# Convolution blocks of a streaming encoder trunk in halves: their matmul form, their order, their banks, and the decay differences on GpSimd

## The chip, the cores and the metric

One core of one Trainium2 chip, one launch. The metric is the device time of the launch in microseconds (us). The kernel is written against the engines directly: every engine has its own instruction stream, and semaphores order them. TensorE is PE in the profile, VectorE DVE, ScalarE ACT, GpSimd POOL, SyncE SP.

## What is computed

A trunk of four layers on 256 tokens of width 1024, all float32, with a memory of 256 tokens. Layers 0 and 3 have a state-space mixer, layer 1 differential attention, layer 2 spatial gating; each has cross attention to the memory beside its mixer, and a feed-forward part behind it:

```python
for i in range(DEPTH):
    h = rmsnorm(x, norm_mix[i])
    proj = h @ w_in                       # mixer input and the cross queries
    mix_out = mixer(proj)                 # by the kind of layer
    cross = memory_cross_attention(xq, mem_n, w_mem_kv[i], ...)
    x = x + jnp.concatenate([mix_out, cross], axis=-1) @ w_out
    x = x + squared_relu_mlp(rmsnorm(x, norm_ffn[i]), w_ff1[i], w_ff2[i])

def mamba2_mixer(proj, ...):
    z, xbc, dt = jnp.split(proj, ...)     # 2048, 4096, 32 columns
    xbc = jax.nn.silu(causal_depthwise_conv(xbc, conv_w, conv_b))   # 4 taps
    xs, bm, cm = jnp.split(xbc, ...)      # 2048, 1024, 1024
    dt = jax.nn.softplus(dt + dt_bias)
    y = ssd_chunked(xs, dt, a, bm, cm) + d_skip * xs
    return grouped_rmsnorm(y * silu(z))

def segsum_exp(a):                        # inside ssd_chunked
    cs = jnp.cumsum(a, axis=-1)
    return jnp.exp(jnp.where(mask, cs[..., :, None] - cs[..., None, :], -jnp.inf))
```

The convolution runs along the tokens, over 4096 channels: 32 tiles of 128 channels. The differences of `cs` under the exponential are what "decay differences" means below.

## The kernel before, in words

**Weights as a stream.** All weights come in 569 units of 512 KB (128 partitions x 1024 numbers) and one small dt unit. For each unit SP issues a DMA into the ring `raw` (6 slots), ACT casts it into `w_hi_t` (ring of 4, L1434), DVE subtracts to make the low part `w_lo_t` (L1678), and PE multiplies. Each float32 product is a sum of three matmuls: high by high, high weight by low activation, low weight by high activation. All partial sums stand in PSUM, 8 banks of 128 x 512 numbers: stream blocks take the pairs (0, 1) and (2, 3) in turn, small work takes one of the banks 4 to 7.

**Three forms of a unit.** *nat* (L1229 to L1240) gives tokens on partitions: 2 K tiles x 2 token tiles x 3 products = 12 matmuls of 128x512 a unit. *feat* (L1241 to L1249), used for the convolution blocks alone, gives channels on partitions: 2 K tiles x 4 channel tiles x 3 products = 24 matmuls of 128x256 a unit. *wide* (L1250 to L1266), used by the first feed-forward product, has the high and the low activations side by side in `hT2`, so that one 128x512 matmul gives high by high in the left half of a bank and high by low in the right half, and a 128x256 one adds low by high: 8 + 8 matmuls a unit. Every form moves 6144 columns a unit.

**The order of the work.** The class `Plan` writes one list of steps before the kernel is built; each engine's stream is that list, cut to its own part. `unit` (L224) adds a weight unit, and threads (Python generators) place small steps between units: `yield n` waits n units, `yield n, "kind"` waits on while that kind's engine is estimated to be late (`is_late`, by the table `COST`: ACT, DVE and PE time of each step). `stream_job` takes the next bank pair and forces steps to be placed until its former contents have been read.

**A convolution block** (`conv_block` in `ssm`, 8 a layer, 4 units each, 512 channels) fills one bank pair. Step "conv", once for each half of the block: ACT writes tap 0 with the bias from PSUM into `xsT` or `bcT` (two Identity operations 128x256, L1537), and DVE adds the other three taps from PSUM (six SCALAR_TENSOR_TENSOR, L1761). The pair is free when DVE is through with the second half. Then "silu" on ACT, and for the xs blocks "xs_turn", transposes on PE.

**The decay differences** ("ssd_gap", 8 groups a layer) are 8 TENSOR_SCALAR of 128x128 a group on DVE (L1791) on data that a DMA brings. POOL makes dt ("dt_soft", L1132 to L1148), `xdt` and `xs` weights ("ssd_xd", L1149 to L1162) and the reciprocal roots of the norms.

**Around it.** The blocks of a state-space layer have a fixed order (the tuple in `ssm`: bc16, bc24, xs0, z0, xs1, ...). `key(0, 0)`, the first key block of the memory, takes the pair (0, 1), which value block 0 has to leave first. `head` does a cross attention head: x_score, x_exp, x_norm, x_turn, x_out. `out_projection` goes over its tiles and, for each, over the two column halves `a` and `b`.

Of the kernel before, what the change touches and what calls it, by code (L numbers as in the profile page):

```python
# [53 lines left out]
for _name, _w in (("norm_mix", DEPTH * 8), ("norm_ffn", DEPTH * 8), ("mem_norm", 8), ("xq", DEPTH * 2), ("xk", DEPTH * 2),  # L54
# [14 lines left out]
    "evac": (1.2, 0, 0), "conv": (1.0, 2.7, 0), "silu": (1.1, 0, 0), "xs_turn": (1.2, 0, 0.9), "dt": (0, 0.4, 0), "dt_turn": (0.3, 0.7, 0.2),  # L69
    "dt_soft": (0, 0.8, 0), "decay": (0.3, 0, 0.4), "ssd_gap": (0, 1.7, 0), "ssd_xd": (0, 0, 0), "ssd_a": (1.5, 0.6, 0.65), "ssd_m": (0, 1.8, 0), "ssd_b": (0, 0.85, 2.2),  # L70
# [41 lines left out]
class Plan:  # L112
# [3 lines left out]
    def __init__(self):  # L116
# [6 lines left out]
        self.low_later = self.ticks = 0  # L123
        self.norm_ahead = False
# [97 lines left out]
    def unit(self, form, src, weight, job, first, last, part, at=None, nf=0, then=None):  # L222
# [12 lines left out]
        self.work(1.06, 1.23 * on, {"feat": 2.88, "wide": 2.78}.get(form, 2.72))  # L235
# [77 lines left out]
    def key(self, i, n):  # L313
        self.normed("mem", ("w_mem_kv", i), n * COLS, 2, ("m", self.r_m), "kT", n, ("xk", i))
# [18 lines left out]
    def head(self, i, h):  # L333
# [150 lines left out]
    def out_projection(self, i, l, kind, order):  # L484
# [68 lines left out]
    def ssm(self, i, l):  # L553
# [32 lines left out]

        def conv_block(ft):
            job = self.stream_job(True, True)

            def taps():  # L590
                if 0 < ft < 16:
                    self.until(lambda: ft // 4 - 1 in xs_act)
                self.step("conv", l=l, ft=ft, half=0, job=job, n=self.count("conv"))
                self.spawn(silu(job, ft))
            self.block("feat", "hT", w, DIN + ft * P, job, taps)
# [72 lines left out]
        for what, k in (("bc", 16), ("bc", 24), ("xs", 0), ("z", 0), ("xs", 1), ("bc", 20), ("z", 1), ("bc", 28), ("q", 0), ("xs", 2), ("z", 2),  # L668
# [166 lines left out]
def bass_trunk(nc, A, out):  # L835
    plan = Plan()
    steps, NU = plan.steps, len(plan.units)
    ctx = ExitStack()
    with ctx:
# [59 lines left out]
        xsT = sb("xsT", [P, 4, SEQ], F32, o_s1)  # L899
# [1120 lines left out]
```

## Time and profile before

| what | us |
| --- | --- |
| median of 3 runs (1770.59 to 1770.93) | 1770.88 |
| the profiled execution | 1770.17 |
| its span | 1768.40 |
| PE busy | 1760.0 |
| DVE busy | 1182.3 |
| ACT busy | 1005.3 |
| POOL busy | 220.0 |

The profiled execution is 0.71 us under the median, and 1.77 us of its time lie outside the span. There are 26013 instructions. "Busy" is the union of an engine's instructions; a matmul's own length in the timeline (0.28 us for 128x256) overlaps its neighbours', so the pace of PE is read from the distance of starts, and a row marked "xN" holds N instructions from its start on. A number in square brackets at the end of a timeline row is the idle time before the instruction, and what ended it.

### The profile page before, as it was taken

What the parts mean: (1) busy time and instruction counts of PE and PEld (TensorE: products, weight loads), DVE (VectorE), ACT (ScalarE), POOL (GpSimd) and SP (SyncE); (2) the same over time, 40 slices, a digit from 0 to 9 for tenths busy, and PEclk for the clock granted to TensorE, in tenths of its full rate; (3) what the DMA queues carried; (4) which work ended last, traced back from release to release, by engine and by line L of the source; (5) the groups of instructions that cost most, each with busy time, mean ns of one, the idle gap of its engine ahead of it and who ended that gap; (6) DMA issues with size and microseconds to landing.
All of it is one profiled execution on the core that took longest, in us unless ns stands there. A gap on an engine that the chain in (4) does not pass through costs nothing.

```text
span 1768.4 us, 26013 instructions
## 1 busy us (share of the span) xinstructions
PE 1760.0 (100%) x9556; PEld 1518.9 (86%) x9556; DVE 1182.3 (67%) x1628; ACT 1005.3 (57%) x1598; POOL 220.0 (12%) x548
## 2 busy tenths in 40 slices
PE   9999999999999999999999999999999999999999
PEld 8998988888888888888888888888899998888887
DVE  5788876666665666656566566655678887656665
ACT  6667775544455675544465545444566777545443
POOL 2412231000012220000012300000131223100000
PEclk9999999999999999999999999999999999999999
DMA  7555543555555443555565445555557554355554
GB/s 271 171 204 186 179 143 122 181 190 191 191 186 180 156 141 121 177 191 191 191 213 180 160 136 182 191 191 191 190 168 215 177 173 150 122 190 189 191 191 143
DMA packets 90041, 314.03 MB, mean 178 GB/s; under 512 B 10176, under 2 KB 11584, under 8 KB 89920
## 3 DMA queue, kind: packets, MB, share of 16 engines
q1 hardware_dynamic: 89328, 311.27, 53.0%
q8 instruction: 80, 1.31, 0.3%
q10 hardware_dynamic: 592, 1.12, 0.2%
q14 instruction: 41, 0.34, 0.1%
HBM read 311.23 MB, written 1.11 MB: 177 GB/s over the span
## 4 chain that ended last, share of the span: by engine, by line
PE 96%; DVE 3%; ACT 1%; issue 1%; ACTq 0%; DVEq 0%
PE ps L1236 19%; PE ps L1238 19%; PE ps L1237 19%; PE ps L1258 13%; PE ps L1265 7%; PE ps L1247 3%; PE ps L1248 3%; PE ps L1249 3%; PE ps L1283 1%; PE ps L1383 1%; PE ps L1334 1%; PE ps L1293 1%; DVE w_lo_t L1678 1%; DVE xsT L1761 1%; DVE bcT L1761 1%
## 5 line engine op out<-in xcount | busy, mean ns | idle before, releaser
L1678 DVE TENSOR_TENSOR w_lo_t<-raw,w_hi_t 128x1024 fp32r<-128x1024 f32 x569 | 691.7, 1225 | 367.6 <-ACT w_hi_t L1434 367.0
L1434 ACT ACTIVATE w_hi_t<-raw 128x1024 fp32r<-128x1024 f32 x569 | 596.9, 1059 | 393.5 <-PE ps L1238 148.5
L1236 PE MATMUL ps<-w_hi_t,act_hi 128*128 128x512 f32 x832 | 327.7, 394 | 0.6 <-issue 0.6
L1237 PE MATMUL ps<-w_lo_t,act_hi 128*128 128x512 f32 x832 | 324.3, 390 | 0.0
L1238 PE MATMUL ps<-w_hi_t,act_lo 128*128 128x512 f32 x832 | 324.1, 390 | 0.0
L1258 PE MATMUL ps<-hT,w_hi_t 128*128 128x512 f32 x1024 | 256.0, 392 | 0.0
L1258 PEld LDWEIGHTS ps<-hT,w_hi_t 128*128 128x128 f32 x1024 | 185.9, 189 | 34.4
L1238 PEld LDWEIGHTS ps<-w_hi_t,act_lo 128*128 128x128 f32 x832 | 156.2, 188 | 33.1
L1236 PEld LDWEIGHTS ps<-w_hi_t,act_hi 128*128 128x128 f32 x832 | 156.4, 188 | 31.6 <-issue 1.0
L1237 PEld LDWEIGHTS ps<-w_lo_t,act_hi 128*128 128x128 f32 x832 | 156.5, 188 | 30.2
L1236 PE MATMUL ps<-w_hi_t,hT 128*128 128x512 f32 x416 | 165.7, 398 | 0.0
L1238 PE MATMUL ps<-w_hi_t,hT 128*128 128x512 f32 x416 | 162.4, 390 | 0.0
L1237 PE MATMUL ps<-w_lo_t,hT 128*128 128x512 f32 x416 | 162.1, 390 | 0.0
L1247 PE MATMUL ps<-hT,w_hi_t 128*128 128x256 f32 x512 | 149.1, 291 | 0.5 <-DVE w_lo_t L1678 0.5
L1265 PEld LDWEIGHTS ps<-hT,w_lo_t 128*128 128x128 f32 x1024 | 139.7, 190 | 10.0
L1249 PE MATMUL ps<-hT,w_lo_t 128*128 128x256 f32 x512 | 144.9, 283 | 0.0
L1248 PE MATMUL ps<-hT,w_hi_t 128*128 128x256 f32 x512 | 144.8, 283 | 0.0
L1265 PE MATMUL ps<-hT,w_lo_t 128*128 128x256 f32 x1024 | 142.8, 282 | 0.0
L1236 PE MATMUL ps<-w_hi_t,memT_hi 128*128 128x512 f32 x252 | 101.5, 403 | 0.9 <-issue 0.8
L1247 PEld LDWEIGHTS ps<-hT,w_hi_t 128*128 128x128 f32 x512 | 98.1, 192 | 2.1 <-issue 1.6
L1248 PEld LDWEIGHTS ps<-hT,w_hi_t 128*128 128x128 f32 x512 | 98.2, 192 | 0.4
L1238 PE MATMUL ps<-w_hi_t,memT_lo 128*128 128x512 f32 x252 | 98.5, 391 | 0.0
(225 smaller groups left out, 2279.2 us busy)
## 6 DMA issues: line engine op xcount, KB each, us to landing
raw<-in_wstream SPq DMA_DIRECT2D x569, 512.0 KB, 3.3
gap<-cs_rows SPq DMA_DIRECT2D x32, 256.0 KB, 4.8
mix<-in_mem SPq DMA_DIRECT2D x4, 256.0 KB, 5.2
x<-in_x SPq DMA_DIRECT2D x1, 1024.0 KB, 9.1
raw<-in_wstream SPq DMA_DIRECT2D x2, 256.0 KB, 4.1
wsT<-in_sgu_wT ACTq DMA_DIRECT2D x1, 512.0 KB, 3.6
sgain<-in_sgu_gain ACTq DMA_DIRECT2D x1, 512.0 KB, 5.9
out<-x SPq DMA_DIRECT2D x1, 512.0 KB, 2.8
```

The costliest lines, as they stand in the source:

```text
L1236: pe.matmul(o, ah, wh[:, n], start=first and c == 0, stop=False)
L1237: pe.matmul(o, ah, wl[:, n], start=False, stop=False)
L1238: mm = pe.matmul(o, al, wh[:, n], start=False, stop=last and c == UK - 1)
L1247: pe.matmul(o, wh[:, n], ah, start=first and c == 0 and f % 2 == 0, stop=False, skip_group_check=True)
L1248: pe.matmul(o, wh[:, n], al, start=False, stop=False, skip_group_check=True)
L1249: mm = pe.matmul(o, wl[:, n], ah, start=False, stop=last and c == UK - 1, skip_group_check=True)
L1258: pe.matmul(o.rearrange("p (a b) -> p a b", a=2), wh[:, n], hT2[:, :, kt, :], start=first and c == 0, stop=False, skip_group_check=True)
L1265: mm = pe.matmul(o[:, 0:SEQ], wl[:, n], hT2[:, 0, kt, :], start=False, stop=last and c == UK - 1, skip_group_check=True)
L1283: mm = pe.transpose(ps[:, bf, f * SEQ + t * P:f * SEQ + (t + 1) * P], src[:, t, (2 * m + f) * P:(2 * m + f + 1) * P], ident)
L1434: act.activation(w_hi_t[:, u % RING, :], raw[:, u % SLOTS, :], ACT.Copy).then_inc(w_hi, 1)
L1678: dve.tensor_tensor(w_lo_t[:, u % SLOTS, :], raw[:, u % SLOTS, :], w_hi_t[:, u % RING, :].bitcast(F32), ALU.subtract)\
L1761: ins = dve.scalar_tensor_tensor(out=dst[:, f, d:SEQ], in0=ps[:, job.banks[h], (f % 2) * SEQ:(f % 2 + 1) * SEQ - d], scalar=col("conv_w", ...
```

## The change

1. The form "feat" goes; a form "half" takes its place. A convolution block is now two halves of 256 channels, each of two units and with a bank pair of its own. A unit is 4 K tiles x 256 channels instead of 2 K tiles x 512, brought by two DMAs of 256 KB from two of the old units, in rows of 1 KB. PE does 8 matmuls of 128x512 (high weight by high and low activations side by side) and 8 of 128x256. There are 512 matmuls fewer in the program.
2. The step "conv" is cut in two. "conv_sum": ACT copies the two right halves (high by low) of the pair into a buffer `cv` (128x512), DVE adds the left halves to it, and the banks are free; then POOL writes tap 0 with the bias from `cv` into `xsT` or `bcT` (two TENSOR_SCALAR 128x256). "conv": DVE's six operations read `cv`, not PSUM. conv_sum is placed with the work of one unit earlier (`w=len(self.units) - 1`).
3. "ssd_gap" runs on POOL, and its cost in the table is 0.
4. The order of the blocks starts with z0; x_out comes two units after x_turn; key(0, 0) uses the banks (6, 7); the out projection begins with both first tiles for `a`, then for `b`.

```diff
-    "evac": (1.2, 0, 0), "conv": (1.0, 2.7, 0), "silu": (1.1, 0, 0), ...
-    "dt_soft": (0, 0.8, 0), "decay": (0.3, 0, 0.4), "ssd_gap": (0, 1.7, 0), ...
+    "evac": (1.2, 0, 0), "conv_sum": (0.65, 0.7, 0), "conv": (0, 2.7, 0), "silu": (1.1, 0, 0), ...
+    "dt_soft": (0, 0.8, 0), "decay": (0.3, 0, 0.4), "ssd_gap": (0, 0, 0), ...
...
     def key(self, i, n):
-        self.normed("mem", ("w_mem_kv", i), n * COLS, 2, ("m", self.r_m), "kT", n, ("xk", i))
+        self.normed("mem", ("w_mem_kv", i), n * COLS, 2, ("m", self.r_m), "kT", n, ("xk", i), (6, 7) if i == n == 0 else None)
...
         self.step("x_turn", n=n, job=pT)
-        yield 1, "x_out"
+        yield 2, "x_out"
...
-        for n in range(last):
+        for n, nb in ((0, 0), (1, 0), (0, 1), (1, 1)):
+            unit(n, (a, b)[nb], nb, False, None)
+        for n in range(2, last):
...
+        def half_summed(ft, half, job):
+            if 0 < ft < 16 and half == 0:
+                self.until(lambda: ft // 4 - 1 in xs_act)
+            n = self.count("conv")
+            self.until(lambda: n < 3 or self.n.get("taps", 0) >= n - 2)
+            job.read_act(self)
+            job.read_dve(self)
+            self.step("conv_sum", w=len(self.units) - 1, l=l, ft=ft, half=half, job=job, n=n, xs_free=...)
+            self.spawn(taps(ft, half, n))
...
-        for what, k in (("bc", 16), ("bc", 24), ("xs", 0), ("z", 0), ("xs", 1), ("bc", 20), ("z", 1), ("bc", 28), ("q", 0), ("xs", 2), ("z", 2),
+        for what, k in (("z", 0), ("bc", 16), ("bc", 24), ("xs", 0), ("z", 1), ("xs", 1), ("bc", 20), ("bc", 28), ("xs", 2), ("q", 0), ("z", 2),
                         ("xs", 3), ("q", 1), ("z", 3), ("v", 0), ("v", 1)):
...
             def weights(u):
+                if u in plan.halves:
+                    first, h = plan.halves[u]
+                    c = slice(h * 2 * P, (h + 1) * 2 * P)
+                    for k in range(2):
+                        at = slice(k * UK * 2 * P, (k + 1) * UK * 2 * P)
+                        sp.dma_start(raw[:, u % SLOTS, at].rearrange("p (c f) -> p c f", c=UK),
+                                     A["wstream"][first + k].rearrange("p (c f) -> p c f", c=UK)[:, :, c]).then_inc(raw_in[u % SLOTS], 16)
+                    return
...
@@ the stream of POOL @@
+                elif k == "conv_sum":
+                    pool.wait_ge(dve_free, s["job"].dve)
+                    if s["xs_free"]:
+                        pool.wait_ge(act_free, s["xs_free"])
+                    for f in range(2):
+                        ins = pool.tensor_scalar(dst[:, 2 * h + f, :], cv[:, h, f, :], col("conv_w", c), col("conv_b", ...),
+                                                 ALU.mult, ALU.add)
+                    ins.then_inc(conv_tap, 1)
+                elif k == "ssd_gap":
+                    pool.wait_ge(act_free, s["decay"])
+                    pool.wait_ge(gap_in[n % 2], 32 * (n // 2 + 1))
+                    for b in range(TT):
+                        for h in range(HPG):
+                            ins = pool.tensor_scalar(at_h, at_h, cs[:, c:c + 1], 0.0, ALU.subtract, ALU.min)
+                        ins.then_inc(gap_new, 1)
...
@@ the stream of PE @@
+                    elif s["form"] == "half":
+                        for q in range(4):
+                            for f in range(2):
+                                pe.matmul(o.rearrange("p (a b) -> p a b", a=2), wh[:, n], hT2[:, :, s["at"] + q, :], ...)
+                        for q in range(4):
+                            for f in range(2):
+                                mm = pe.matmul(o[:, 0:SEQ], wl[:, n], hT2[:, 0, s["at"] + q, :], ...)
...
@@ the stream of ACT @@
+                elif k == "conv_sum":
+                    act.wait_ge(job_done, job.done)
+                    if s["n"] > 2:
+                        act.wait_ge(conv_done, s["n"] - 2)
+                    act.activation(cv[:, s["half"], :, :], ps[:, b:b + 2, SEQ:2 * SEQ], ACT.Copy).then_inc(act_free, 1)
...
@@ the stream of DVE @@
+                elif k == "conv_sum":
+                    dve.wait_ge(act_free, job.act)
+                    dve.tensor_tensor(c, ps[:, b:b + 2, 0:SEQ], c, ALU.add).then_inc(dve_free, 1)
                 elif k == "conv":
+                    dve.wait_ge(conv_tap, s["n"])
                     for d in range(1, TAPS):
-                        for f in (2 * h, 2 * h + 1):
-                            ins = dve.scalar_tensor_tensor(out=dst[:, f, d:SEQ], in0=ps[:, job.banks[h], ...],
+                        for f in range(2):
+                            ins = dve.scalar_tensor_tensor(out=dst[:, 2 * h + f, d:SEQ], in0=cv[:, h, f, 0:SEQ - d], scalar=col("conv_w", c),
```

Three places show how the order moves. The first is PE, the first unit of a convolution block in the program (these three rows come once for each of its 2 K tiles and 4 channel tiles). Before:

```order
L1247 MATMUL ps<-hT,w_hi_t 128x256
L1248 MATMUL ps<-hT,w_hi_t 128x256
L1249 MATMUL ps<-hT,w_lo_t 128x256
```

With the change, two units of the first half:

```order
L1292 MATMUL ps<-hT,w_hi_t 128x512 x8
L1297 MATMUL ps<-hT,w_lo_t 128x256 x8
L1292 MATMUL ps<-hT,w_hi_t 128x512 x8
L1297 MATMUL ps<-hT,w_lo_t 128x256 x8
```

A unit's 24 matmuls of 128x256 have become 8 of 128x512 and 8 of 128x256.

The second place is DVE, from the last operation of the dt chain on into the first convolution block (bc16) of layer 0. `cv` is the new buffer, `percol_sb` holds the tap weights. Before:

```order
L1783 RECIPROCAL xdt<-xdt 128x64 [waits dve_chain]
L1678 TENSOR_TENSOR w_lo_t<-raw,w_hi_t 128x1024 [waits w_hi] x2
L1761 SCALAR_TENSOR_TENSOR bcT<-ps,percol_sb,bcT 128x255 [waits conv_in]
L1761 SCALAR_TENSOR_TENSOR bcT<-ps,percol_sb,bcT 128x255
L1761 SCALAR_TENSOR_TENSOR bcT<-ps,percol_sb,bcT 128x254 [waits dve_chain]
L1761 SCALAR_TENSOR_TENSOR bcT<-ps,percol_sb,bcT 128x254
L1761 SCALAR_TENSOR_TENSOR bcT<-ps,percol_sb,bcT 128x253 [waits dve_chain]
L1761 SCALAR_TENSOR_TENSOR bcT<-ps,percol_sb,bcT 128x253
L1678 TENSOR_TENSOR w_lo_t<-raw,w_hi_t 128x1024 [waits w_hi]
```

With the change:

```order
L1829 RECIPROCAL xdt<-xdt 128x64 [waits dve_chain]
L1724 TENSOR_TENSOR w_lo_t<-raw,w_hi_t 128x1024 [waits w_hi] x4
L1800 TENSOR_TENSOR cv<-ps,cv 128x512 [waits act_free]
L1724 TENSOR_TENSOR w_lo_t<-raw,w_hi_t 128x1024 [waits w_hi]
L1808 SCALAR_TENSOR_TENSOR bcT<-cv,percol_sb,bcT 128x255 [waits conv_tap]
L1808 SCALAR_TENSOR_TENSOR bcT<-cv,percol_sb,bcT 128x255
L1808 SCALAR_TENSOR_TENSOR bcT<-cv,percol_sb,bcT 128x254 [waits dve_chain]
L1808 SCALAR_TENSOR_TENSOR bcT<-cv,percol_sb,bcT 128x254
L1808 SCALAR_TENSOR_TENSOR bcT<-cv,percol_sb,bcT 128x253 [waits dve_chain]
L1808 SCALAR_TENSOR_TENSOR bcT<-cv,percol_sb,bcT 128x253
L1724 TENSOR_TENSOR w_lo_t<-raw,w_hi_t 128x1024 [waits w_hi]
L1800 TENSOR_TENSOR cv<-ps,cv 128x512 [waits act_free]
```

The taps wait for POOL (conv_tap) instead of ACT (conv_in); an add stands ahead of them, with a weight subtraction between it and them.

The third place is POOL, from the end of dt_soft on into the first groups of layer 0 (`dt_keep` is dt, `xdt` and `xs` are the weighted inputs, the numbers behind `gap` are buffers). Before:

```order
L1148 TENSOR_SCALAR dt_keep<-xdt 128x64
L1157 TENSOR_TENSOR xdt<-xs,dt_keep 128x256 x2
L1161 TENSOR_TENSOR xs<-xs,rows_sb 128x256 x2
L1157 TENSOR_TENSOR xdt<-xs,dt_keep 128x256 x2
L1161 TENSOR_TENSOR xs<-xs,rows_sb 128x256 x2
```

With the change:

```order
L1174 TENSOR_SCALAR dt_keep<-xdt 128x64
L1184 TENSOR_SCALAR bcT<-cv,percol_sb 128x256 x8
L1184 TENSOR_SCALAR xsT<-cv,percol_sb 128x256 x4
L1194 TENSOR_SCALAR gap_83<-gap_83,cs 128x128 x4
L1194 TENSOR_SCALAR gap_84<-gap_84,cs 128x128 x4
L1204 TENSOR_TENSOR xdt<-xs,dt_keep 128x256 x2
L1208 TENSOR_TENSOR xs<-xs,rows_sb 128x256 x2
L1194 TENSOR_SCALAR gap_85<-gap_85,cs 128x128 x4
L1194 TENSOR_SCALAR gap_86<-gap_86,cs 128x128 x4
L1184 TENSOR_SCALAR xsT<-cv,percol_sb 128x256 x2
L1204 TENSOR_TENSOR xdt<-xs,dt_keep 128x256 x2
```

Between dt_soft and the weighting of the inputs POOL now has the taps of six halves and the differences of two groups, and further taps (`xsT`, x2) stand behind the differences of the next.

## Rows read from the trace of the kernel before

**Rows 1.** The page: busy time, granted clock, chain by engine.

```profile
PE 1760.0 (100%) x9556; PEld 1518.9 (86%) x9556; DVE 1182.3 (67%) x1628; ACT 1005.3 (57%) x1598; POOL 220.0 (12%) x548
...
PEclk9999999999999999999999999999999999999999
...
PE 96%; DVE 3%; ACT 1%; issue 1%; ACTq 0%; DVEq 0%
```

**Rows 2.** Waits, engine PE: waited for, us in total, times, longest us.

```profile
PE ps L1392 <- DVE xp L1910: 0.6, 2, 0.3
...
PE ps L1247 <- DVE w_lo_t L1678: 0.5, 2, 0.2
```

**Rows 3.** Timeline of PE, 58.9 to 62 us: start us, us; 24 matmuls of one unit.

```profile
58.99 0.28 PE L1247 MATMUL ps<-hT,w_hi_t 128*128 128x256 f32 x1
...
61.75 0.28 PE L1249 MATMUL ps<-hT,w_lo_t 128*128 128x256 f32 x1
```

**Rows 4.** Timeline of PE, 340 to 344.3 us: wide units of a feed-forward stage.

```profile
340.65 2.00 PE L1258 MATMUL ps<-hT,w_hi_t 128*128 128x512 f32 x8
...
342.49 1.12 PE L1265 MATMUL ps<-hT,w_lo_t 128*128 128x256 f32 x8
...
343.44 1.09 PE L1258 MATMUL ps<-hT,w_hi_t 128*128 128x512 f32 x4
```

**Rows 5.** Timeline of PE around four waits, with idle time and its releaser.

```profile
30.32 0.39 PE L1238 MATMUL ps<-w_hi_t,memT_lo 128*128 128x512 f32 x1
31.54 0.47 PE L1236 MATMUL ps<-w_hi_t,memT_hi 128*128 128x512 f32 x1 [0.82 <-issue]
...
277.70 0.39 PE L1238 MATMUL ps<-w_hi_t,act_lo 128*128 128x512 f32 x1
279.00 0.36 PE L1404 MATMUL ps<-xpT,v 128*128 128x256 f32 x1 [0.91 <-DVE xpT_lo L1915]
...
299.81 0.39 PE L1238 MATMUL ps<-w_hi_t,act_lo 128*128 128x512 f32 x1
300.48 0.63 PE L1392 MATMUL ps<-consts_sb,xp 128*128 128x128 f32 x4 [0.28 <-DVE xp L1910]
...
1509.86 0.39 PE L1238 MATMUL ps<-w_hi_t,memT_lo 128*128 128x512 f32 x1
1510.43 0.36 PE L1404 MATMUL ps<-xpT,v 128*128 128x256 f32 x1 [0.18 <-issue]
```

**Rows 6.** Timeline of DVE, 29 to 32 us.

```profile
30.03 1.41 DVE L1922 SCALAR_TENSOR_TENSOR v_lo<-ps,stats,v 128x512 fp32r<-128x512 f32 x2 [3.13 <-ACT v L1529]
```

**Rows 7.** Timeline of DVE, 71 to 79 us: one half of a convolution block.

```profile
72.19 2.69 DVE L1761 SCALAR_TENSOR_TENSOR bcT<-ps,percol_sb,bcT 128x255 f32<-128x255 f32 x6 [1.48 <-ACT bcT L1537]
74.79 1.22 DVE L1678 TENSOR_TENSOR w_lo_t<-raw,w_hi_t 128x1024 fp32r<-128x1024 f32 x1
75.92 2.68 DVE L1761 SCALAR_TENSOR_TENSOR bcT<-ps,percol_sb,bcT 128x255 f32<-128x255 f32 x6
```

**Rows 8.** Groups by line and shape, engine DVE: busy us, mean ns, idle before.

```profile
L1937 DVE TENSOR_TENSOR rf<-ps,rf 128x512 f32<-128x512 f32 x64 | 41.2, 686 | 45.5 <-ACT rf L1641 45.5
...
L1791 DVE TENSOR_SCALAR gap<-gap,cs 128x128 f32<-128x128 f32 x128 | 32.9, 328 | 0.0
```

**Rows 9.** POOL: line L1157 (ns min/median/max), and timeline, 70 to 92 and 1301 us.

```profile
L1157 POOL TENSOR_TENSOR xdt<-xs,dt_keep x32: 606/612/1685, 109.1 to 1473.6; 128x256 f32<-128x256 f32 x32
...
81.28 0.37 POOL L1148 TENSOR_SCALAR dt_keep<-xdt 128x64 f32<-128x64 f32 x1
...
1301.65 0.25 POOL L1138 TENSOR_SCALAR xdt<-xdt 128x64 f32<-128x64 f32 x1
```

**Rows 10.** Waits, engine DVE, 58 to 335 us, the first state-space stage.

```profile
DVE w_lo_t L1678 <- ACT w_hi_t L1434: 41.3, 31, 3.2
```

**Rows 11.** DMA issues: KB each, median us to landing.

```profile
raw<-in_wstream SPq DMA_DIRECT2D x569, 512.0 KB, 3.3
...
mix<-in_mem SPq DMA_DIRECT2D x4, 256.0 KB, 5.2
```

More of the change, by code:

```diff
@@ L123, in __init__ @@
         self.low_later = self.ticks = 0
+        self.halves = {}
         self.norm_ahead = False
@@ L234, in unit @@
         self.lo_n.append(self.n_lo[on])
-        self.work(1.06, 1.23 * on, {"feat": 2.88, "wide": 2.78}.get(form, 2.72))
+        self.work(1.06, 1.23 * on, {"half": 2.78, "wide": 2.78}.get(form, 2.72))
         w = {0: 1 - AHEAD, 1: 2 - AHEAD, 2: 3 - AHEAD, 3: 2}.get(u, u)
@@ L302, in row_norm, with normed @@
             self.threads.insert(0, self.turning)
-    def normed(self, src, weight, col, groups, r, dst, n, gain):
-        job = self.stream_job(True, True)
+    def normed(self, src, weight, col, groups, r, dst, n, gain, banks=None):
+        job = Job(self, banks, True, True) if banks else self.stream_job(True, True)
         self.block("nat", src, weight, col, job, lambda: self.row_norm(job, groups, r, dst, 4 * n, gain))
@@ L571, in ssm, with taps @@
         self.norm_ahead = True
-        def silu(job, ft):
+        def taps(ft, half, n):
             yield 1, "conv"
-            job.read_act(self)
-            job.read_dve(self)
-            self.step("conv", l=l, ft=ft, half=1, job=job)
+            self.step("conv", l=l, ft=ft, half=half, n=n, tap_n=self.count("taps"))
+            if half == 0:
+                return
             yield 2, "silu"
             conv[ft] = self.count("silu")
-            self.step("silu", ft=ft, dve=job.dve)
+            self.step("silu", ft=ft, taps=n)
             if ft < 16:
@@ L585, in silu @@
                 xs_act[ft // 4] = jobs[-1].act
-        def conv_block(ft):
[L588 to L595, printed above, removed]
+        def half_summed(ft, half, job):
[5 more added lines that the diff above has]
+            job.read_dve(self)
+            self.step("conv_sum", w=len(self.units) - 1, l=l, ft=ft, half=half, job=job, n=n, xs_free=xs_act[ft // 4 - 1] if 0 < ft < 16 else 0)
+            self.spawn(taps(ft, half, n))
+        def conv_block(ft):
+            u0 = len(self.units)
+            for half in range(2):
+                job = self.stream_job(True, True)
+                for n in range(2):
+                    u = len(self.units)
+                    self.halves[u] = (u0 + 2 * n, half)
+                    self.unit("half", "hT", (w, 2 * UK * half + UK * n, DIN + ft * P), job, n == 0, n == 1, self.parts["hT"][2 * n + 1], 4 * n,
+                              then=(lambda: half_summed(ft, half, job)) if n else None)
         def rows(g):
@@ L837, in bass_trunk @@
     steps, NU = plan.steps, len(plan.units)
+    landed = []
+    for u in range(NU):
+        landed.append((landed[u - SLOTS] if u >= SLOTS else 0) + (2 if u in plan.halves else 1))
     ctx = ExitStack()
@@ L1424, in cast_to @@
                     u = cast[0]
-                    act.wait_ge(raw_in[u % SLOTS], 16 * (u // SLOTS + 1))
+                    act.wait_ge(raw_in[u % SLOTS], 16 * landed[u])
                     if u >= RING:
```

65 lines of the change are left out of this document (25 added, 40 removed).

## The prediction, as made before the changed kernel ran

> **What bounds the kernel now.** I read the page first, then PE's waits, then timelines. The page says that PE is busy for 1760.0 of 1768.4 us at a granted clock of nine tenths or more in all 40 slices, and that the chain which ended last is 96% PE [rows 1]. The reader is to see there that only two things can shorten the span: a shorter path through PE's own matmuls, or the few places where PE stands still. PE's waits are small: the largest named groups sum to 0.6 and 0.5 us [rows 2]. So the timeline around them matters more than the sums. A matmul's modelled length overlaps its neighbour's, so I read the distance of starts: 0.23 us is the normal step of a 128x512 matmul (1.84 us for 8 [rows 4]), and what a step has over that is the stall.
>
> **The pace of PE.** In the "feat" form the 24 starts of a unit reach from 58.99 to 61.75, 23 steps of 0.120, so a unit takes 2.88 us [rows 3]. The "wide" form, whose pattern the new "half" form copies, takes 1.84 for eight 128x512 and 0.95 for eight 128x256, 2.79 in all [rows 4]. Both move 6144 columns. Two layers x 8 blocks x 4 units = 64 units: 64 x (2.88 - 2.79) = **-5.8 us**, on the path, since PE never rests there. Behind the row: the Trainium skill ("TensorE: Matmul & The Clock Gate", on the gap of isolated matmuls) puts a matmul at N/2.4 GHz plus some 2.5 ns. By it the two forms would stand at 24 x 109.2 = 2.62 and 8 x 215.8 + 8 x 109.2 = 2.60 us, and the gain would be an estimated 1.3 us. The trace's 0.120 and 0.230 disagree with it, and the sum goes by the trace.
>
> **Banks and orders.** Three stalls go.
> - The first key block waits for banks (0, 1): its first start is 31.54, 1.22 us behind the one before, 0.99 over a normal step [rows 5]. What holds it is DVE reading them for v_lo, from 30.03 to 31.44 [rows 6]. On banks (6, 7) it needs nobody: **-1.0**.
> - x_out of a head waits for the low part of its transposed probabilities: 277.70 to 279.00, 1.07 too much, and 1509.86 to 1510.43, 0.34 too much [rows 5]. With two units between x_turn and x_out (2 x 2.76 us) DVE has the time: **-1.4**.
> - x_turn waits for xp at 299.81, 0.44 too much, and twice in all by the waits [rows 2, 5]. With the new order of the blocks and of the out projection's first units other small work stands ahead of it: 2 x 0.44 = **-0.9**. This is the least sure of the three; the other end is 0.
>
> The sum so far is -9.1. With the profiled execution's 1770.17, which stands 0.71 under the median, that would be 1761.1, or 1761.8 beside the median.
>
> **What leaves and enters DVE, ACT, POOL and the queues.** DVE loses the 128 differences, 8 x 0.33 = 2.6 us a group [rows 8], and gains two adds a block; an add of 128x512 from PSUM takes 0.69 [rows 8]. ACT loses two of its four operations a block. The two loads of a half unit come in rows of 1 KB; the nearest row, a 256 KB load in such rows, took 5.2 us to land against 3.3 for a whole unit [rows 11]. Two of them side by side may take 5.2 to 10.4; the ring holds six units, and a unit is consumed in 2.79, so five units ahead are 14 us. Both ends cost nothing. SP issues 64 DMAs more, 128 in place of 64 over 180 us; nothing there is near.
>
> **The new wait.** This is the price of the change. For each half DVE has to do an add (0.69), two weight subtractions (74.79 to 75.92, 1.13 each) and six taps (72.19 to 74.79, 2.60) [rows 7, 8]: 5.55 us against PE's 2 x 2.79 = 5.58. It is balanced to the hair, and only if DVE never waits. But the order is add, subtraction, taps, and the taps wait for POOL's two operations, which can start only after the add. If they run beside the subtraction, they are hidden: two of 0.4 to 0.6 us [rows 9] in 1.13. If POOL cannot read SBUF beside that subtraction, it starts behind it, and DVE idles some 1.1 us a half. For the second: line L1157 has a median of 0.61 and a maximum of 1.685 [rows 9], so POOL's operation is at times held for 1.07 us, about one subtraction.
>
> Take it as held. The first taps also wait for POOL's dt chain, which now runs 81.65 - 1.0 (the key wait gone) = 80.65 before it is free [rows 9]; two taps of 0.55 and DVE starts at 81.75. It then needs 2.60 + 1.13 until the low part for unit 27 is there, 85.5, and PE comes to that unit at 58.99 + 4 x 2.76 + 6 x 2.79 + 0.9 for small groups = 87.7 [rows 3, 4]. So there is a cover of 2.2 us. Five further halves in the same stretch (bc16, bc24, xs0 back to back) lose 1.1 each, 5.5: 3.3 over the cover. The second stretch (xs1, bc20, bc28, xs2, eight halves) starts with more lead and costs some 1.0. The bounds are 0 and 4.3 a layer, 0 and 8.6 in two. I take 1.8 a layer, **+3.6**: toward 0 from the upper end, because in this stage DVE now idles 41.3 us waiting for ACT's casts in 31 places [rows 10], and ACT is the engine that is relieved. If that cover were gone, the price would be the full 8.6.
>
> **Sum.** 1770.17 - 9.1 + 3.6 = 1764.7; beside the median 0.71 more: **1765.4**.
>
> **Rivals.**
> - *The full lag.* POOL is held in each half and nothing is made up: 1761.8 + 8.6 = 1770.4, no change. For it: the 5.55 against 5.58. Against it: the relief on ACT [rows 10].
> - *No pace to be gained.* The steps of 0.230 and 0.120 hold in their own stages, and the half form runs at 2.88 for its 6144 columns: 1765.4 + 5.8 = 1771.2. Against it: the weights' layout is the same as in the wide stage [rows 4]. This also covers the case that the change does not do what its text says.
> - *Slower: POOL's differences hold the taps.* A group's eight differences take 0.35 each if nothing holds them; held each time for 1.07, 11.4 us [rows 8, 9]. In POOL's order they stand ahead of an xs half's taps, DVE stands in its wait for them, and its weight subtractions are queued behind. PE can run on for one and a half units, 4.2 us; 7.2 a layer is left, 1761.8 + 14.4 = 1776.2. It decides from 12.6 us for both layers, 6.3 a layer. For it: 1.685 occurs, and a tensor_scalar 128x64 on POOL took 0.25 alone at 1301.65, 0.37 at 81.28 [rows 9]. Against it: the median is 0.61, so most operations on POOL are not held. By the Trainium skill ("SBUF — State Buffer", who interferes with whom) a VectorE operation with two SBUF inputs and a GpSimd one that reads SBUF exclude each other for the whole instruction. The trace agrees with it in the maximum alone, and the six taps, which now read two SBUF tensors instead of one, would by it lock POOL out as well.
>
> **How the numbers follow.** A measurement of this kernel tells about 0.2% from no change, 3.5 us: the borders are 1767.3 and 1774.4. The forecast has 0.68 (its own range is 1762 to 1768), the full lag 0.14, no pace gain 0.04, the slower rival 0.14. That gives faster 0.68, same 0.18, slower 0.14. The range reaches from 1760.5 (nothing is lost, and some stalls of DVE go besides) to 1772, which takes in the full lag and leaves out the slower case and a little below.
>
> **What would show it.** Right: PE's steps in the half form at 0.230 and 0.120; no stall at the first key block; DVE's idle time ahead of the taps about 1 us where POOL is named, with PE's waits for w_lo_t at the first and the second stretch near 1.8 us a layer together; POOL's taps at 0.4 to 0.6 us but starting when a subtraction ends. Wrong: PE waiting more than 6 us a layer for w_lo_t; POOL's differences in lengths of 1.4 us; ACT or the landing of the 1 KB rows named as what ends PE's or DVE's waits; a unit of the half form at 2.88 us or more.

## The result: 55 us slower, all of it in the two state-space stages

The changed kernel took 1826.10 us (median of 4 runs, 1825.71 to 1826.49) against 1770.91 beside it: a ratio of 1.0312, 95% interval 1.0299 to 1.0326. The prediction had 1765.4 in a range of 1760.5 to 1772. It was wrong in sign and by 61 us.

The page of the profile after, the lines that answer to [rows 1], and those of the decay differences and of the half loads:

```profile
PE 1773.1 (97%) x9044; PEld 1501.8 (82%) x9044; DVE 1184.8 (65%) x1532; ACT 987.7 (54%) x1562; POOL 411.5 (23%) x740
...
PEclk9999989999999999999999999999999999999999
...
L1194 POOL TENSOR_SCALAR gap<-gap,cs 128x128 f32<-128x128 f32 x128 | 136.0, 1079 | 24.2 <-DMA gap<-cs_rows 24.2
...
raw<-in_wstream SPq DMA_DIRECT2D x130, 256.0 KB, 3.5
```

PE is no longer busy all the time: 1773.1 of 1824.6 us, and its busy time has even grown by 13 us with 512 matmuls fewer. That is one sign of a slower clock; the sixth slice of PEclk is the other. POOL has gone from 220.0 to 411.5 us. The half loads land in 3.5 us and are no matter.

Where the time went is told by the first and last weight load of the wide line, before (L1258) and after (L1307):

```profile
L1258 PEld LDWEIGHTS ps<-hT,w_hi_t x1024: 187/188/193, 334.0 to 1741.5; 128*128 128x128 f32 x171
```
```profile
L1307 PEld LDWEIGHTS ps<-hT,w_hi_t x1024: 187/188/192, 368.9 to 1798.1; 128*128 128x128 f32 x171
```

The first marks the end of layer 0's mixer stage: 34.9 us late. The last lies in layer 3's feed-forward stage: 56.6 late. The layers between have the same form in both kernels, so the second state-space stage lost the other 21.7.

PE's waits, the largest (for: us in total, times, longest):

```profile
PE ps L1292 <- DVE cv L1800: 12.5, 4, 5.0
PE ps L1283 <- DVE w_lo_t L1724: 7.9, 5, 3.6
PE ps L1332 <- ACT mix L1631: 7.7, 2, 3.8
```

Before, the largest were 1.5 (behind "issue"), 1.1 (behind `nt`) and 0.9 (behind `xpT_lo`); [rows 2] leaves these out, and the prediction's "largest named groups" of 0.6 and 0.5 are not the largest. The 15 groups after sum to 48 us. As a check I summed, over all PE matmuls, what each distance of starts has over the median distance of its line: steps more than 0.4 us too long hold 51.2 us after and 4.1 before; the small excesses 27.1 and 10.8; and the medians themselves sum to 1741.6 and 1748.5. So the stalls cost +47.1, slow steps +16.3 (14.7 of it while the granted clock is 0.50), and the pace gave -6.9: 56.5 together, against the 56.2 us by which the span grew.

By place, of the 51.2 us of large stalls 0.5 stands at the start, 4.8 stand in and just behind the first stretch of halves of the two layers, 20.5 in and just behind the second (10.3 and 10.2), and 25.3 later, ahead of xs_turn, at the turns of `mix` and at the out projection (18.1 and 7.2).

**The slow steps** stand behind the stalls. The timeline of PE at the start of the out projection, and the stretches around it (us, PE busy, granted clock, DMA share, GB/s):

```profile
258.05 1.09 PE L1332 MATMUL ps<-consts_sb,mix 128*128 128x128 f32 x4 [3.83 <-ACT mix L1631]
262.96 0.76 PE L1283 MATMUL ps<-w_hi_t,act_hi 128*128 128x512 f32 x1 [3.83 <-DVE act_lo L1775]
...
263.95 0.63 PE L1285 MATMUL ps<-w_hi_t,act_lo 128*128 128x512 f32 x1
264.38 0.63 PE L1283 MATMUL ps<-w_hi_t,act_hi 128*128 128x512 f32 x1
```
```profile
254.00:260.00 6.00, 1.30 (x5) 0.79 0.27 87
260.00:264.00 4.00, 1.04 (x3) 0.50 0.01 2
264.00:270.00 6.00, 6.00 (x26) 0.69 0.01 3
```

After two idle stretches of 3.83 us the granted clock is 0.50, the lower level of 1.2 GHz, and a 128x512 matmul steps at 0.43 instead of 0.23. So a stall costs more than its length here: the one at 144 us is 4.9, with 1.5 of slow steps behind it.

**Two terms of the sum can be read off directly.** The pace, and the wait for POOL's taps. PE, then DVE, in the first stretch of halves:

```profile
90.91 2.00 PE L1292 MATMUL ps<-hT,w_hi_t 128*128 128x512 f32 x8
92.75 1.12 PE L1297 MATMUL ps<-hT,w_lo_t 128*128 128x256 f32 x8
93.71 2.00 PE L1292 MATMUL ps<-hT,w_hi_t 128*128 128x512 f32 x8
```
```profile
101.73 2.70 DVE L1808 SCALAR_TENSOR_TENSOR bcT<-cv,percol_sb,bcT 128x255 f32<-128x255 f32 x6 [1.00 <-POOL bcT L1184]
104.35 1.22 DVE L1724 TENSOR_TENSOR w_lo_t<-raw,w_hi_t 128x1024 fp32r<-128x1024 f32 x1
105.48 0.68 DVE L1800 TENSOR_TENSOR cv<-ps,cv 128x512 f32<-128x512 f32 x1
106.09 1.22 DVE L1724 TENSOR_TENSOR w_lo_t<-raw,w_hi_t 128x1024 fp32r<-128x1024 f32 x1
108.31 2.70 DVE L1808 SCALAR_TENSOR_TENSOR xsT<-cv,percol_sb,xsT 128x255 f32<-128x255 f32 x6 [1.00 <-POOL xsT L1184]
```

A half unit takes 93.71 - 90.91 = 2.80, as forecast. DVE idles 1.00 us ahead of each half's taps, where 1.1 was forecast, and its cycle is 108.31 - 101.73 = 6.58, against PE's 2 x 2.80 = 5.60. What the sum left to a rival is in the next rows, POOL's and DVE's; the first row is POOL's taps in the first stretch, the others stand in the second:

```profile
99.77 1.93 POOL L1184 TENSOR_SCALAR bcT<-cv,percol_sb 128x256 f32<-128x256 f32 x2 [4.65 <-DVE cv L1800]
...
116.99 8.98 POOL L1194 TENSOR_SCALAR gap<-gap,cs 128x128 f32<-128x128 f32 x8 [2.15 <-DMA gap<-cs_rows]
125.94 1.18 POOL L1204 TENSOR_TENSOR xdt<-xs,dt_keep 128x256 f32<-128x256 f32 x2
127.09 1.18 POOL L1208 TENSOR_TENSOR xs<-xs,rows_sb 128x256 f32<-128x256 f32 x2
128.25 8.41 POOL L1194 TENSOR_SCALAR gap<-gap,cs 128x128 f32<-128x128 f32 x8
136.66 1.08 POOL L1184 TENSOR_SCALAR xsT<-cv,percol_sb 128x256 f32<-128x256 f32 x2
```
```profile
137.77 4.76 DVE L1808 SCALAR_TENSOR_TENSOR xsT<-cv,percol_sb,xsT 128x255 f32<-128x255 f32 x6 [5.05 <-POOL xsT L1184]
```

A group's differences hold POOL for 8.4 to 9.0 us here. On DVE they took 2.1 on the mean, 32.9 us for 16 groups [rows 8]; the prediction's 2.6 adds up durations that overlap. The taps stand behind them, DVE waits 5.05 us, and PE stands until 144.36 for the banks. DVE's six taps then take 4.76 us instead of 2.70, while POOL weights the inputs for the next group (137.71 to 140.03). That is the slower rival's chain, and this last delay besides. But is it the whole of the 55 us?

### The profile page after: what moved, and what is told of

It reads as the page before. It is cut to its first block and busy times, and to the rows that moved or that the text cites. A ratio compares the mean times of both kernels' runs of the same rounds, so it can differ in the third digit from the quotient of the medians.

```text
span 1824.6 us, 25195 instructions
## 1 busy us (share of the span) xinstructions
PE 1773.1 (97%) x9044; PEld 1501.8 (82%) x9044; DVE 1184.8 (65%) x1532; ACT 987.7 (54%) x1562; POOL 411.5 (23%) x740
## 5 line engine op out<-in xcount | busy, mean ns | idle before, releaser
L1307 PE MATMUL ps<-hT,w_hi_t 128*128 128x512 f32 x1024 | 256.0, 392 | 0.0
L1307 PEld LDWEIGHTS ps<-hT,w_hi_t 128*128 128x128 f32 x1024 | 185.9, 189 | 34.4
L1292 PE MATMUL ps<-hT,w_hi_t 128*128 128x512 f32 x512 | 134.6, 406 | 12.8 <-DVE cv L1800 12.5
L1314 PE MATMUL ps<-hT,w_lo_t 128*128 128x256 f32 x1024 | 142.8, 282 | 0.0
L1194 POOL TENSOR_SCALAR gap<-gap,cs 128x128 f32<-128x128 f32 x128 | 136.0, 1079 | 24.2 <-DMA gap<-cs_rows 24.2
L1292 PEld LDWEIGHTS ps<-hT,w_hi_t 128*128 128x128 f32 x512 | 94.3, 192 | 31.9 <-issue 13.7
L1283 PEld LDWEIGHTS ps<-w_hi_t,hT 128*128 128x128 f32 x416 | 79.0, 190 | 26.9 <-issue 11.5
```

Source lines behind the costliest of these rows:

```text
L1194: ins = pool.tensor_scalar(at_h, at_h, cs[:, c:c + 1], 0.0, ALU.subtract, ALU.min)
L1283: pe.matmul(o, ah, wh[:, n], start=first and c == 0, stop=False)
L1292: pe.matmul(o.rearrange("p (a b) -> p a b", a=2), wh[:, n], hT2[:, :, s["at"] + q, :], start=first and q == 0, stop=False, skip_group_chec ...
L1307: pe.matmul(o.rearrange("p (a b) -> p a b", a=2), wh[:, n], hT2[:, :, kt, :], start=first and c == 0, stop=False, skip_group_check=True)
L1314: mm = pe.matmul(o[:, 0:SEQ], wl[:, n], hT2[:, 0, kt, :], start=False, stop=last and c == UK - 1, skip_group_check=True)
```

## The experiments

Theory 1 was that rival. Rival 2: the taps on POOL. Rival 3: the new order of the blocks. Differences and taps can each be put back alone. Medians stand beside runs of the kernel before on the same chip (1770.43 to 1770.95).

One thing goes with most of these runs. Moving the differences or tap 0 changes their entries in the table of costs (the differences 0 on POOL, 1.7 on DVE), so `Plan` writes another list of steps: in e1 and in e3 some 300 of the 1256 places hold another step than in the changed kernel. Such a run shows engine and list together; no run moves the differences with the list held fixed. The lists of e1, e4 and e11 are the same step for step, and so are those of e6, e9 and e12, so what tells these apart is the work alone.

### e1_gap_dve: differences back on DVE

```diff
-                elif k == "ssd_gap":   # in POOL's stream
+                elif k == "ssd_gap":   # in DVE's stream, the same eight operations; COST (0, 1.7, 0)
```

> The changed kernel with the decay differences back on DVE, at their old place and planner cost; all else as changed. Theory 1 (the differences on POOL, 8.5 us a group, hold POOL's taps and the state-space chain; the long stalls of PE and the slow clock behind them are theirs): the 4 to 5 us stalls go, 1762 to 1770 us. Rival 2 (the taps on POOL behind the add are the cause, the differences only stand near): 1810 us or more, stalls at conv blocks stay. Rival 3 (the new block order leaves the out projection without cover): the stalls before the out projection stay, about 1795 us.

1809.08 us (ratio 1.0217, 1.0202 to 1.0232). Theory 1 and rival 3 are off, and rival 2's "1810 us or more" is missed by 0.9; e3 tests it. The differences on POOL, with the list of steps that goes with them, cost 1826.1 - 1809.1 = 17 us, near the 14.4 of the slower rival, but 38 us remain.

### e2_before_gap_pool: the kernel before, differences on POOL

> The kernel before with the decay differences on POOL and nothing else. Theory 1: no taps on POOL here, so only the state-space chain is late: a group every 13 us or so against the mixing of POOL and DVE, stalls ahead of the out projection as in the changed kernel, 25 to 35 us slower, 1796 to 1806 us. Rivals 2 and 3: 1771 to 1775 us, since neither taps nor order are changed.

1779.99 us (1.0052, 1.0037 to 1.0067): +9.4. In a kernel without taps on POOL they cost, but about a third of what theory 1 expected, and the rivals had 5 at most. Their line, with the shortest, the median and the longest in ns:

```profile
L1156 POOL TENSOR_SCALAR gap<-gap,cs x128: 708/714/2542, 105.3 to 1490.5; 128x128 f32<-128x128 f32 x128
```

Even the shortest takes 0.71 us on POOL.

### e3_taps_act: tap 0 on ACT, differences on POOL

```diff
+                elif k == "conv":      # in ACT's stream, in place of POOL's part of conv_sum
+                    act.wait_ge(dve_free, s["sum_dve"])
+                    for f in range(2):
+                        ins = act.activation(dst[:, 2 * h + f, :], cv[:, h, f, :], ACT.Identity, bias=..., scale=...)
+                    ins.then_inc(conv_tap, 1)
```

> The changed kernel with tap 0 written by ACT (two Identity operations from the buffer cv, in the step conv) in place of POOL; differences stay on POOL. Theory 1: the conv stalls of 5.0, 1.6 and 3.8 us a layer and the slow clock behind them go, the ones before the out projection stay: about 1798 to 1806 us. Rival 2: 1765 to 1775 us. Rival 3: 1800 us, too.

1799.83 us (1.0166, 1.0149 to 1.0183), where theory 1 and rival 3 had it, and not where rival 2 did. With nothing of the convolution behind them, the differences no longer hold a tap: 26 us less than the changed kernel.

### e4_both: differences on DVE, tap 0 on ACT

> The changed kernel with both: differences on DVE and tap 0 on ACT, so POOL does as little as before. Theory 1: as e1_gap_dve or up to 4 us below it, 1760 to 1766 us, since the idle 1.0 us of DVE ahead of the taps in the back-to-back halves goes, too. If the lag behind POOL's taps costs nothing, equal to e1_gap_dve.

1801.03 us (1.0172, 1.0157 to 1.0187). Theory 1 had 1760 to 1766, so it is only half: POOL does what it did before, and 30 us are still lost. With the taps on ACT, differences on POOL (e3) and on DVE (e4) come out alike (1.2 us apart, within the intervals). The timelines of DVE, ACT and PE at the new largest stall:

```profile
155.03 5.30 DVE L1797 SCALAR_TENSOR_TENSOR bcT<-cv,percol_sb,bcT 128x255 f32<-128x255 f32 x12
160.25 0.68 DVE L1789 TENSOR_TENSOR cv<-ps,cv 128x512 f32<-128x512 f32 x1
```
```profile
157.82 0.60 ACT L1564 ACTIVATE cv<-ps 128x512 f32<-128x512 f32 x1 [4.43 <-DVE bcT L1797]
```
```profile
161.04 3.75 PE L1271 MATMUL ps<-hT,w_hi_t 128*128 128x512 f32 x8 [5.63 <-DVE cv L1789]
```

The taps of two halves run in one piece (x12, 5.30 us): the planner had put them off as it took DVE to be late (those of bc20's first half by four units, where one is the least), until the two-slot buffer `cv` forced them. ACT's copy of the next half waits for a slot, DVE's add for the copy, and PE for the banks that only the add frees.

### e5_old_order and e6_old_order_gap_dve: the old order of the blocks

```diff
-        for what, k in (("z", 0), ("bc", 16), ("bc", 24), ("xs", 0), ("z", 1), ("xs", 1), ("bc", 20), ("bc", 28), ("xs", 2), ("q", 0), ("z", 2),
+        for what, k in (("bc", 16), ("bc", 24), ("xs", 0), ("z", 0), ("xs", 1), ("bc", 20), ("z", 1), ("bc", 28), ("q", 0), ("xs", 2), ("z", 2),
```

> The changed kernel with the blocks in the order of before (bc16, bc24, xs0, z0, xs1, bc20, z1, ...); differences and taps stay on POOL. e4_both showed stalls of 5.8 and 3.9 us where eight halves stand back to back beside the first groups. Theory A (DVE is the bound in that stretch; put-off taps are forced two at a time and hold the buffer cv, the copy and the banks): those stalls shrink, what is left is POOL's part, 17 us by e1 against the changed kernel, so 1785 to 1800 us. Theory B (the halves themselves with their two-slot buffer cost it wherever they stand): 1815 us or more.

> The order of before and the differences on DVE; half form, cv and taps on POOL as changed. Theory A: 1765 to 1778 us, stalls under 1.5 us each. Theory B: near e1_gap_dve's 1809 us.

e5: 1802.09 us (1.0178, 1.0164 to 1.0191). e6: 1814.30 us (1.0248, 1.0234 to 1.0262). e5 lies between the two theories, e6 5 us above what theory B had. In the changed kernel itself the order is worth much: the old order alone makes it 1826.1 - 1802.1 = 24.0 us faster. The large stalls late in the two stages go from 25.3 us to 4.0 (in e5 those behind 200 and 1450 us), which is what rival 3, the out projection without cover, would have. This is the wait for the turns of `mix`, 7.7 us in the changed kernel, in e5:

```profile
PE ps L1332 <- ACT mix L1631: 1.5, 2, 0.8
```

With the differences on DVE it is the other way: the old order is 5 us worse than the new one. Theory A fell there, and rival 3 is no whole explanation, since the halves cost in either order:

| halves, with | new order | old order |
| --- | --- | --- |
| differences and taps on POOL | 1826.1 (the change) | 1802.1 (e5) |
| differences on DVE, taps on POOL | 1809.1 (e1) | 1814.3 (e6) |
| differences on POOL, taps on ACT | 1799.8 (e3) | not run |
| differences on DVE, taps on ACT | 1801.0 (e4) | 1809.3 (e9) |

Moving the differences to POOL helps by 12 us in the old order where it hurt by 17 in the new one, as it would if DVE had too much to do there. On DVE they also take longer beside POOL's 128x256 operations (e6, DVE, then POOL; at 118.75 POOL is idle):

```profile
118.75 1.65 DVE L1828 TENSOR_SCALAR gap<-gap,cs 128x128 f32<-128x128 f32 x8
...
164.27 3.53 DVE L1828 TENSOR_SCALAR gap<-gap,cs 128x128 f32<-128x128 f32 x8
```
```profile
164.21 1.22 POOL L1184 TENSOR_SCALAR bcT<-cv,percol_sb 128x256 f32<-128x256 f32 x2 [14.13 <-DVE cv L1791]
165.40 1.18 POOL L1195 TENSOR_TENSOR xdt<-xs,dt_keep 128x256 f32<-128x256 f32 x2
166.54 1.18 POOL L1199 TENSOR_TENSOR xs<-xs,rows_sb 128x256 f32<-128x256 f32 x2
```

### e7_before_new_order: the order alone

> The kernel before with the new order of the blocks and nothing else. Theory A, if the order alone loads DVE too much: 1780 to 1795 us. If it needs the halves' add and the two-slot buffer as well: within 5 us of 1771. Theory B: 1771 us.

1793.22 us (1.0128, 1.0114 to 1.0141): without a single half, the order alone costs 22.8 us. Its longest stall is 3.36 us at 189 us, where the third xs block and q0 now meet the first groups; I read the chain behind it no further.

### e8_before_small: the three small edits alone

> The kernel before with the three small edits alone: first key block on banks (6, 7), x_out two units behind x_turn, the first four units of the out projection in the new order. By the prediction's terms the stalls of 0.99, 1.07 and 0.34 us go, perhaps 0.44 twice: 1767.3 to 1768.3 us. The rival is that the stalls only move: 1770.6 us.

1766.07 us (0.9974, 0.9964 to 0.9984), 9 runs against 13: 4.4 us faster than before, and the fastest kernel of the study. That is 1.2 us under the range. The stalls at the key block, at x_out and for xp are gone; those over 0.4 us are down from 4.1 us to 1.2 in all. PE's largest waits now, of which the first two stood there before:

```profile
PE ps L1191 <- DVE nt L1684: 1.1, 1, 1.1
PE ps L1249 <- DVE w_lo_t L1680: 0.5, 2, 0.2
PE ps L1238 <- DVE w_lo_t L1680: 0.5, 2, 0.3
```

### e9 to e12: load or latency?

The stalls of e6 stand at places other than e4's: 67 us and 195 us, each where halves follow a norm block (key 1, q0). Theory C: a half uses its pair for two units, so the pair of the block ahead is wanted back after 5.6 us; before it was 11.5. A norm block's pair is free only after ACT's squares, POOL's root and DVE's product.

> Halves with the order of before, tap 0 on ACT, differences on DVE: e6_old_order_gap_dve without POOL's taps. Theory C (halves turn the bank pairs over in two units instead of four, so whatever a norm block leaves in its pair must be read within 5.6 us; the first key's successor and q0 stand ahead of halves in this order): the stalls near 67 us and 195 us and their repetition in layer 3 stay, 1800 to 1812 us. Theory D (POOL's held taps are the main cost): under 1785 us.

> Halves, tap 0 on ACT, differences on DVE, and an order in which each norm block (key 1, q0, q1) is followed by a z block and at most three conv blocks stand together: z0 bc16 bc24 xs0 z1 xs1 bc20 q0 z2 bc28 xs2 xs3 q1 z3. Theory C with the DVE bound: 1778 to 1792 us, below e4_both's 1801, with what is left in the stretch bc28 xs2 xs3. Theory D: 1801, as e4_both.

> e4_both with the taps at distances 1 and 2 left out (DVE does 2 of the 6 operations of a half; the convolution is then incomplete). If DVE is the bound in the long stretch of halves (theory A): its 5.8 and 3.9 us stalls and most of the ones before the out projection go, 1763 to 1775 us. If the stalls are latencies of chains through ACT and banks: 1790 us or more.

> e9_old_both with the same taps left out. Theory C: the stalls behind the norm blocks (near 67 and 195 us) are latency, not DVE's load, and stay at 2.5 us or more each with the slow clock behind them: 1780 to 1795 us, above e11_new_few_taps. If only DVE's load counts: equal to e11_new_few_taps.

The edit of e11 and e12, which leave the taps at distances 1 and 2 out of the convolution:

```diff
-                    for d in range(1, TAPS):
+                    for d in range(TAPS - 1, TAPS):
```

| run | order | us | ratio (interval) |
| --- | --- | --- | --- |
| e9_old_both | old | 1809.33 | 1.0217 (1.0202 to 1.0233) |
| e10_mixed_order | mixed | 1826.00 | 1.0311 (1.0296 to 1.0327) |
| e11_new_few_taps | new | 1787.03 | 1.0092 (1.0077 to 1.0107) |
| e12_old_few_taps | old | 1800.99 | 1.0173 (1.0156 to 1.0190) |

Against e6, e9 shows what POOL's taps cost with the differences on DVE and the same list of steps: 5.0 us in the old order, and 8.1 in the new (e1 against e4). e10 is a miss: 1778 to 1792 was expected, and the mixed order is the worst of the three and as slow as the changed kernel. PE waits 7.59 us for the silu of an xs block and 6.16 for the evacuation of a z block. Ahead of the first DVE works off the taps of three halves (205.29 to 217.65), of which the planner had put one off by four units; ahead of the second ACT stands 5.58 us for DVE's `cbm`. No run takes either chain apart. An order that looks balanced by blocks says nothing of either. e11 shows the load: with four of six operations gone, and all else in the same order, the 5.63 us stall shrinks to 0.5, and the time by 14.0. At 1787.03 it still misses theory A's 1763 to 1775, so load on DVE is about half of what is lost in e4. e12, with 1801 above the range of theory C too, shows that in the old order this load is the smaller part: 8.3 us less, and the stalls behind the norm blocks stay (6.52 us, after 7.84 in e9). PE, DVE and ACT of e12 at the second:

```profile
188.89 1.62 PE L1271 MATMUL ps<-hT,w_hi_t 128*128 128x512 f32 x3 [6.52 <-issue]
```
```profile
185.77 1.22 DVE L1713 TENSOR_TENSOR w_lo_t<-raw,w_hi_t 128x1024 fp32r<-128x1024 f32 x1 [3.90 <-ACT w_hi_t L1462]
186.91 0.68 DVE L1789 TENSOR_TENSOR cv<-ps,cv 128x512 f32<-128x512 f32 x1
187.51 1.28 DVE L1784 TENSOR_TENSOR nt<-ps,stats 128x512 f32<-128x512 f32 x2
```
```profile
178.73 1.28 ACT L1602 ACT_TABLE_LOAD   x1
180.02 1.15 ACT L1602 ACTIVATE E<-gap 128x512 f32<-128x512 f32 x2
181.08 0.26 ACT L1606 ACTIVATE cb<-ps 128x128 f32<-128x128 f32 x1
181.36 1.28 ACT L1578 ACT_TABLE_LOAD   x1
182.66 1.06 ACT L1578 ACTIVATE bcT<-bcT 128x1024 f32<-128x1024 f32 x1
...
184.68 1.06 ACT L1462 ACTIVATE w_hi_t<-raw 128x1024 fp32r<-128x1024 f32 x1
```

"issue" hides the releaser: PE starts 0.1 us after DVE's product for the norm (`nt`, 187.51 to 188.79), which has q0's banks. DVE came to it late because it idled 3.90 us for a cast, and ACT came late to that cast because an exponential, a silu and two table loads of 1.28 us stood ahead. DVE is not overloaded there. ACT is the one without a gap, from 176.19 us to 186.22; it is a chain through three engines, and the pair is wanted before it ends.

### e14_same_pair and e15_same_pair_gap_pool: the pairs alone

```diff
             for half in range(2):
+                if half and ft in (16, 8):
+                    self.pair ^= 1
                 job = self.stream_job(True, True)
```

> e9_old_both, but the second half of the two blocks that follow a norm block (bc16 after key 1, xs2 after q0) takes the bank pair of its own first half instead of the norm block's, so the norm chain has four units again; in exchange that half must wait for its predecessor's copy and add, about 1.5 to 2 us each. Theory C: the stalls of 2.9 us (67 us) and 8.0 us (191 us) give way to ones of about 1.5 to 2.5 us, with less slow clock, twice a run: 1790 to 1798 us against 1809. If the turnover of the pairs is not the cause: 1809 us or more.

> The same with the differences on POOL (tap 0 stays on ACT, so POOL's differences hold no taps). DVE is relieved by 1.65 to 3.5 us a group; POOL is slower at it, so the state-space chain is later. If DVE's load decides with the pairs mended: 5 to 12 us below e14_same_pair. If the chain's latency decides: no gain.

e14: 1801.69 us (1.0174, 1.0159 to 1.0190), 7.6 under e9, where 1790 to 1798 had been expected. The first stall shrank from 2.78 to 1.46 us, and PE now waits for the buffer's copy, as it should. PE of e14:

```profile
65.62 2.08 PE L1273 MATMUL ps<-hT,w_hi_t 128*128 128x512 f32 x8 [1.46 <-ACT cv L1566]
...
188.09 3.75 PE L1273 MATMUL ps<-hT,w_hi_t 128*128 128x512 f32 x8 [5.34 <-issue]
```

The second went from 7.84 to 5.34 only: ACT, behind two table loads, is as late for the copy (186.03) as it was for the cast, DVE's add ends at 187.98, and PE starts 0.1 us later. So the turnover is shown at the first place, and is a part of the second. e15: 1794.13 us (1.0131, 1.0114 to 1.0147): with no taps behind them and the pairs mended, the differences on POOL, with their list of steps, save 7.6 us, within the 5 to 12 that load on DVE would give.

## Why the prediction was wrong, step by step

- **The pace of PE: right.** 2.80 us a half unit; the medians of the steps sum to 6.9 us less, 5.8 were forecast. The rule of isolated matmuls, N/2.4 GHz plus 2.5 ns (the Trainium skill, "TensorE: Matmul & The Clock Gate", on the back-to-back issue gap), would have had an estimated 1.3; the steps of 0.23 disagree again.
- **Banks and orders: right, 1.1 short.** -3.3 forecast, -4.4 measured in e8.
- **DMA: right**, no cost; 3.5 us to landing.
- **POOL's taps held by the subtraction: right** (1.1 us a half forecast, 1.00 measured). DVE's lead took a part of it: in the first stretch PE's stalls are 0.4, 0.9, 0.5 and 1.0, 2.8 us in layer 0, within the 3.3 that the prediction allowed. e4, where ACT writes the tap, has none of them.
- **"The second stretch [...] starts with more lead and costs some 1.0": wrong; this is the step that failed.** In the changed kernel PE's large stalls there are 10.3 us in layer 0 and 10.2 in layer 3. One cause is POOL's chain above. The other is that I never added up DVE's work. Eight halves take 8 x 5.55 = 44.4 us of DVE, and two groups of the state-space chain stand in the same stretch. Each brings DVE, by the rows of e1 to e9, cbm 0.42, the differences 1.65, xw 0.42, E 1.29, xs 0.87, and 1.6 for cbm, xs and mix: 6.2 us, 12.5 for two, 56.9 in all. PE's halves there take 16 x 2.79 = 44.6, but the groups' own matmuls come on top: at their median steps PE's work in that stretch of e4 is 51.7 us. So DVE has some 5 us too many, about 10%, even if it never waits. e11 takes 8 x 1.73 = 13.9 us off DVE in each layer's stretch; its large stalls there go from 6.9 to 0.7 us in layer 0 and from 5.2 to 0.7 in layer 3. The whole run gained 14.0 us where 27.7 of DVE's work went from both stretches.
- **Behind the second stretch the sum has no term at all.** 25.3 of the 51.2 us of large stalls stand there. e5 shows that the new order makes most of them while differences and taps are on POOL. By which chain, no run shows.
- **"Two units later the banks are wanted again" was in the code and not in the sum.** The forecast priced what the halves do themselves, not what they ask of the block ahead. The old order has norm blocks ahead of halves, the new one mends that and puts four convolution blocks in a row. In the old order the wait behind the norm block is shown by e14 (2.78 us down to 1.46 at the first place). Either way the halves cost: +43.9 with the old order (e6), +38.5 with the new (e1), small edits and pace gain already in them.
- **The slower rival (0.14) had the right mechanism for its part**: 14.4 forecast, 17 by e1. That the sizes are near is partly luck. One difference was too short (0.35 us each, from operations of half the size; 0.70 is the shortest, 1.08 the mean) and the hold of each too long, so a group's 11.4 stands against 6.3 to 10.6 measured; and the 17 hold the other list of steps as well. The rule behind it (the Trainium skill, "SBUF — State Buffer", who interferes with whom) is borne out: POOL's two taps take 1.93 us behind a subtraction (99.77) and 1.08 without one (136.66), and DVE's six taps 4.76 instead of 2.70 beside POOL's weighting (137.77). DVE's eight differences, which have one such input, go from 1.65 to 3.53 us beside POOL's operations in e6. By the same section a VectorE tensor_scalar in a two-port mode also excludes GpSimd, which would fit; that these run in that mode no run shows.
- **The cover was misread.** DVE's 41.3 us of waiting for casts [rows 10] looked like slack. It is not free time at a chosen moment. ACT's casts wait in turn for PE, 25.4 us in 12 places in the same window before, so much of it is latency of the chain from PE's release of a slot. In the changed kernel's first state-space stage (70 to 369 us) DVE still waits 46.8 us for casts, in 29 places, and the stalls came all the same.
- **The slow clock was in no case**: 16 us of slow steps. With stalls at 1.3 times their length, as here, even the right list of stalls would have been short.
- **A part of the edit that does nothing.** `w=len(self.units) - 1` for conv_sum leaves the order of ACT's casts and DVE's subtractions as it is without it, by the kernel's own code: the matmul step ahead has already asked for the same casts. Banks are freed sooner by the copy and the add alone.

What stays open: the effects don't add. Taking POOL's part out (e4) gives back 25 of the 55 us, and most of DVE's taps besides (e11) another 14; the other 16 are not taken apart. The order costs 22.8 with full blocks and 24.0 in the changed kernel, but with the differences on DVE it is 5 to 8 us better than the old one, and why is not shown. The stalls of 3.7 to 4.0 us ahead of xs_turn and at the out projection in e11 were not taken apart by a run; the trace shows table loads and put-off steps ahead of them. Not tried either: taps that the planner never puts off, a third slot in `cv`, and the differences on the other engine with the list of steps unchanged.

## What to carry to other kernels

When a step is cut in halves, add up each engine's work over the densest stretch, with everything else that the schedule puts there, and the bounding engine's as well; an average of 65% busy hides a stretch that asks for 10% more than there is. Ask of every buffer that turns over faster who had it last, and how long that one's chain of readers is, through all engines. Try each part of a change alone: here 4.4 us of gain were buried under 60 of loss, and the order alone cost 23. And where a planner reads a table of costs, a changed entry moves other steps, too.

## What the hardware showed that was not expected

- In this kernel the stalls of PE cost about a third more than their length (16.3 us of slow steps to 47.1 of stalls): after two of 3.83 us idle the granted clock was 0.50 and 128x512 steps were 0.43 us instead of 0.23.
- A two-operation tensor_scalar on GpSimd took 0.71 us for 128x128 (subtract, min) but 0.54 to 0.56 for 128x256 (multiply, add): the size alone does not set it. DVE does the first in 0.21 where POOL is idle, 0.44 beside POOL's 128x256 operations.
- Loads of 256 KB in rows of 1 KB landed in 3.5 us, in contrast to 5.2 for the rows of [rows 11].
